# A fourth group of query weights ahead of the first weighted sum, loaded into two row buffers

## The reference

```python
q = (xt @ w_query).reshape(T, PEER_HEADS, 2, PEER_KEY_DIM // 2)   # 256 tokens, 8 heads, 2 x 128
s = jnp.einsum('thcd,hckd->thck', q, sub_keys)                    # 128 keys per half
s_top, i_top = lax.top_k(s, PEER_TOPK)                            # 16 of each half
...
g_s, g_pos = lax.top_k(cand, PEER_TOPK)                           # 16 of the 256 sums
g = jax.nn.softmax(g_s, -1)
# per token, head and choice: one row of expert_u and one of expert_v, 1024 numbers each
h = gelu(einsum('td,thkd->thk', xb, expert_u[eb]))
y = einsum('thk,thkd->td', g * h, expert_v[eb])
```

## Time and profile before

| | |
|---|---|
| median of the runs | 960.07 us |
| profiled execution | 959.62 us, its span 957.8 us |
| PE busy | 761.8 us (80%) |
| DVE busy | 593.0 us (62%) |
| ACT busy | 426.3 us (45%) |
| POOL busy | 300.8 us (31%) |
| mean granted TensorE clock | 0.839 |
| bytes moved by DMA | 335.33 MB |

### The profile page before, as it was taken

How to read it: one execution, slowest core, us unless ns; L and a number is a source line. 1 busy time by engine, 2 the same in 40 slices (tenths; PEclk the granted TensorE clock), 3 DMA queues, 4 the chain that set the end, 5 groups by cost and what they waited for, 6 DMA issues and landing times.

```text
span 957.8 us, 11712 instructions
## 1 busy us (share of the span) xinstructions
PE 761.8 (80%) x4022; PEld 352.5 (37%) x4026; DVE 593.0 (62%) x1424; ACT 426.3 (45%) x1179; POOL 300.8 (31%) x296
## 2 busy tenths in 40 slices
PE   7999999998888989979695757676867665767664
PEld 6876755665633435433131404141411111111110
DVE  1615340643779878868566655677667766767555
ACT  1144213542268967965343424354443434334333
POOL 0010021000334634544333334344433433343430
PEclk9999999999979997989796869697976777566667
DMA  7533253625799999999999999999999999999993
GB/s 280 238 119 122 100 230 144 257 85 231 280 420 420 420 422 401 420 420 423 420 422 422 421 421 422 421 419 422 421 420 423 420 419 423 421 421 420 420 421 151
DMA packets 45645, 335.33 MB, mean 350 GB/s; under 512 B 6033, under 2 KB 6033, under 8 KB 9105
## 3 DMA queue, kind: packets, MB, share of 16 engines
q0 software_dynamic: 37152, 268.45, 67.6%
q1 hardware_dynamic: 8432, 66.13, 17.5%
HBM read 333.51 MB, written 1.05 MB: 349 GB/s over the span
## 4 chain that ended last, share of the span: by engine, by line
DMA 45%; PE 36%; DVE 9%; ACT 5%; issue 3%; POOL 2%; SPq 0%; POOLq 0%; DVEq 0%; ACTq 0%
DMA late<-in_uv,eidx 27%; DMA ring<-in_uv,eidx 16%; PE ps L715 7%; PE ps L1052 7%; PE ps L700 5%; PE ps L839 4%; PE ps L881 4%; ACT late L1101 3%; DVE late L1804 2%; DVE ring L1804 2%; DMA late<-in_uv,apart 2%; ACT L1101 1%; PE ps L983 1%; POOL late L1903 1%; PE ps L950 1%
## 5 line engine op out<-in xcount | busy, mean ns | idle before, releaser
L1101 ACT ACTIVATE late<-late 128x1 f32<-128x1 f32 (+3 forms) x787 | 221.8, 285 | 337.0 <-DVE late L1804 315.0
L1052 PE MATMUL ps<-late 64*64 64x512 f32 x960 | 168.2, 789 | 77.4 <-ACT late L1101 73.8
L1052 PE MATMUL ps<-ring,late 64*64 64x512 f32 x928 | 162.0, 783 | 82.6 <-ACT late L1101 81.6
L1903 POOL DMA_INDIRECT late<-in_uv,eidx x118 | 130.7, 1107 | 249.5 <-PE ps L1052 183.9
L1804 DVE CUSTOM_DVE_ANT_0 late<-late,x_sb 128x1024 f32<-128x1024 f32 x120 | 147.0, 1225 | 92.7 <-DMA late<-in_uv,eidx 90.8
L1804 DVE CUSTOM_DVE_ANT_0 ring<-ring,x_sb 128x1024 f32<-128x1024 f32 x116 | 142.1, 1225 | 88.3 <-DMA ring<-in_uv,eidx 86.6
L1903 POOL DMA_INDIRECT ring<-in_uv,eidx x116 | 127.6, 1100 | 179.6 <-PE ps L1052 171.1
L1101 ACT ACT_TABLE_LOAD x82 | 105.2, 1283 | 11.8 <-PE ps L700 10.3
L1052 PEld LDWEIGHTS ps<-ring,late 64*64 64x64 f32 x928 | 29.3, 155 | 187.9 <-ACT late L1101 172.8
L1052 PEld LDWEIGHTS ps<-late 64*64 64x64 f32 x960 | 30.9, 156 | 179.5 <-ACT late L1101 161.1
L1101 ACT ACTIVATE tmp<-ps 128x512 f32<-128x512 f32 (+4 forms) x86 | 43.3, 507 | 94.6 <-PE ps L700 41.5
(11 more groups left out here) (254 smaller groups left out, 756.4 us busy)
## 6 DMA issues: line engine op xcount, KB each, us to landing
wring<-in_wts SPq DMA_DIRECT2D x21, 2048.0 KB, 11.4
wring<-in_wts SPq DMA_DIRECT2D x2, 1428.0 KB, 5.7
wring<-in_wts SPq DMA_DIRECT2D x2, 1388.0 KB, 6.3
ring<-in_wts SPq DMA_DIRECT2D x1, 2048.0 KB, 10.3
lnw<-in_ln SPq DMA_DIRECT2D x4, 512.0 KB, 12.5
late<-in_uv,eidx POOLq DMA_INDIRECT x118
ring<-in_uv,eidx POOLq DMA_INDIRECT x116
wring<-in_wts SPq DMA_DIRECT2D x3, 512.0 KB, 7.5
```

The costliest lines, as they stand in the source:

```text
L1052: last = mm(o[t][n * HD:(n + 1) * HD, :], factor[tokens, :], values[tokens, n * 512:(n + 1) * 512], start=start, stop=stop, skip_group_che ...
L1101: return nc.scalar.activation(out, in_, func, **kw)
L1903: G.indirect_dma_start(row(slots[g]), None, uv, bass.IndirectOffsetOnAxis(eidx[:, u % 2, k:k + 1], 0)).then_inc(row_here[slots[g]], 16)
```

## The change

Heads 4 and 5 become one group, (2, 0, 2), and `EARLY` becomes 4, so this group is multiplied ahead of `weighted(0)` too. Its weights no longer pass through `wring`: SP loads them into the whole of `ring2` (buffers 4 and 5), and POOL waits for the end of their multiplication, `("q", 0, OWN_HOME)`, before it issues row 6, the first one into `ring2`; `SLOT_ORDER` makes these two buffers the last of each eight up to g = 160. The two groups left, heads 6 and 7, stand at steps 25 and 42. The list of pieces is one shorter: piece 18 is now heads 6 and 7, piece 19 the first of block 1's output projection.

```diff
-QUERIES = [[(0, 0, 1), (0, 1, 1), (1, 0, 2), (2, 0, 1), (2, 1, 1), (3, 0, 1), (3, 1, 1)], [(n, 0, 2) for n in range(4)]]
-EARLY = 3
+QUERIES = [[(0, 0, 1), (0, 1, 1), (1, 0, 2), (2, 0, 2), (3, 0, 1), (3, 1, 1)], [(n, 0, 2) for n in range(4)]]
+EARLY = 4
+OWN_HOME = 3
+SLOT_ORDER = [0, 1, 2, 3, 6, 7, 4, 5]
...
-    for n, k in enumerate((14, 25, 36, 47)):
+    for n, k in enumerate((25, 42)):
         queries(0, EARLY + n, k, 1, 3)
...
-        slots = [g % RING0 if g < SWITCH else (g - SWITCH + RING0) % RING for g in range(NT * STEPS)]
+        slots = [SLOT_ORDER[g % RING0] if g < SWITCH else (g - SWITCH + RING0) % RING for g in range(NT * STEPS)]
...
-            order += [(18 + n, ("q", i, max(g for g, group in enumerate(QUERIES[i]) if group[0] == n))) for n in range(4)]
+            order += [(18 + n, ("q", i, max(g for g, group in enumerate(QUERIES[i]) if group[0] == n))) for n in range(4) if (i, n) != (0, 2)]
...
+                if k == 19:
+                    sp.wait_ge(sq_ready, NT + 1)
+                    await_full(sp, "qT", 1, 3)
+                    sp.dma_start(ring2[:, :], wts[:, starts[20]:starts[21]]).then_inc(wq_here, 16)
...
-                    if first == 0:
+                    if (i, n) == (0, OWN_HOME):
+                        pe.wait_ge(wq_here, 16)
+                        query[0] = ring2[:, :].rearrange("p (k n) -> p k n", k=KD)
+                    elif first == 0:
                         query[0] = next_piece()
...
+                if g == 4:
+                    await_full(pool, "z", 1, 1)
                 if g == 6:
-                    await_full(pool, "z", 1, 1)
+                    await_full(pool, "q", 0, OWN_HOME)
```

More of the change, by code:

```diff
@@ L478, in layer @@
         wz_here = sem("wz_here")
+        wq_here = sem("wq_here")
         first_step = sem("first_step")
```

## The result

The changed kernel takes 974.94 us, median of 4 runs (973.56 to 976.16), beside 960.37 for the kernel before in the same comparison: a ratio of 1.0157, 95% interval 1.0143 to 1.0171. That is 14.6 us slower. The profiled execution took 975.58, its span 973.7, which is 15.9 us more than before.

What follows compares the result with a forecast made beforehand. It took DMA bytes to bound the kernel from 250 us on; 4.9 (queues dry) + 8.9 (ramp) - 1.5 (clock) - 0.7 (dent) = 11.6 us on 959.62 gave 971.2, stated as 971.5, range 966 to 976 (55%).

Steps and rivals of the forecast that it cites:

- What bounds it: From 250 us on, the kernel ends when its bytes are through; DMA engines move about 420 GB/s.
- more than 421 GB/s anywhere: Sign of a wrong prediction: the DMA engines finding a rate above 421 GB/s at any place.
- The load: SP's load into ring2 behind piece 18: issued at 250.9 us, landing at about 270.1.
- turns of equal bytes: Alternative for SP's and POOL's queues sharing DMA: weights land at 274 us, sum 4 us higher; not taken.
- T: End of heads 4 and 5's queries on PE: 280.0 us, bounds 276.7 and 284.2, queries taking 9.8 us.
- The queues dry: Start of loop: queued bytes through at 277.6 us, row 6's bytes begin at 282.5; 4.9 us idle.
- The ramp: Rows 8 to 11 issued 7.4, 14.7, 18.9 and 20.6 us behind T; 8.9 us of DMA idle.
- I take 1.5: Taken off the ramp: second and third sums and scores partly at full clock, 1.5 of about 3 us.
- The half of the dent: DMA dent at 375 to 386 us, 1.4 us in all, half of it expected back.
- Row 12: Sign in the changed profile: row 12's dot product about 14 us later than before.
- Free by cover: Queries out of steps 14 and 36, output projection's first piece, buffer order and gate's wait at row 4 cost nothing.
- Nothing lost: Rival, 10%: the pauses at the loop's start stay covered, needing T = 267.9; 959 to 961 us.

Runs made afterwards that it cites:

- before_scores_ahead: Kernel before, with only block 1's compressed scores moved from between the first two sums to ahead of the first; 960.56 us, ratio 0.9998.
- warm_wait: Changed kernel plus 40 spare 128x128 matmuls on PE in its wait for the weights; 972.13 us, ratio 1.0121.
- buffer_order_alone: Kernel before, with only the change's order of buffers and the gate's wait at row 4; 960.22 us, ratio 0.9997.
- early_load: Changed kernel with SP's load into ring2 moved ahead of piece 18's wait; 963.24 us, ratio 1.0025.
- scores_in_wait: Changed kernel with block 1's compressed scores moved from step 0 into PE's wait for the weights; 970.21 us, ratio 1.0097.
- ahead_through_wring: Kernel before, with heads 4 and 5 multiplied ahead as one group, weights still through wring, no gather held; 967.01 us, ratio 1.0062.

## Why the prediction was right

The direction, the mechanism and the place hold; the size was 14.6 us where 11.6 was forecast (975 against 971.5).

- *What bounds it.* Right: bytes behind 250 us set the end, and the missing 16.2 us of transfer are the 15.9 us of the span. before_scores_ahead shows the other side of it. One sign of being wrong was met by the letter, "more than 421 GB/s anywhere": from 262 to 276 the changed kernel moves 426, with SP's load beside the rows. That is 0.2 us of work and moves nothing in the sum; 421 is the rate of the long stretch, not the highest that is seen.
- *The load.* Forecast at 250.9 and landed at 270.1; it was 249.5 and 269.6 with the loop 1.4 us earlier, so 0.9 us late. By the measured shares this was close. From 258 to 268 SP's queue (q1) again had about two thirds of the engines; behind each queue stand its packets, its MB and its share:

```profile
q1 hardware_dynamic: 197, 2.79, 65.2%
q0 software_dynamic: 203, 1.48, 35.1%
```

The rule of the Trainium skill, DMA: Bandwidth & Descriptors, "Queues, rings and completion order", that each DMA engine takes turns between its queues by the packet, agrees with this if one counts the profile's packets (which need not be what that page calls a packet): the two queues moved nearly the same number, 197 and 203 here, 109 and 108 before. But SP's packets are about twice as large, 14.2 KB against 7.3 on average here and 16.4 against 7.1 before, so even turns give SP two thirds of the bytes. The landing that the prediction worked out for turns of equal bytes would have been 3 us too late.

- *T.* Forecast 280.0, measured 280.1, in the loop's own time 1.5 us late: 0.9 from the landing, most of the rest from the queries, 10.2 us instead of 9.8. That these two figures lie so near is in part luck. The 8.4 us that the prediction took as the full-clock time hold a pause of 0.9 us that is no work; without it such queries take 7.3. And the clock cost 2.9 us, not 1.4: about half of the rows ran at the lower level and not a quarter (granted 0.50 from 270 to 274, 0.54 to 276, 1.00 behind it). The two errors cancel to 0.4 us.
- *The queues dry* at 277.6 and fed again at 282.5: measured about 276.6 (131 GB/s in the two us from 276) and about 282.7. This pause is 6.1 us where the sum had 4.9, for T was late by 1.5 in the loop's own time.
- *The ramp.* Issues of rows 8, 9, 10 and 11 forecast 7.4, 14.7, 18.9 and 20.6 us behind T, measured 8.0, 16.3, 20.6 and 22.3. The form was right and it was 1.7 us longer, mostly since the compressed scores ran at about 0.50 from their start: 7.0 us instead of 5.9. Idle in it by the prediction's own way of adding are then 10.6 us instead of 8.9, and 10.1 are missed from 284 to 304.
- *The step that failed* is the one taken off the ramp, "I take 1.5", for a better clock behind the queries. The clock was worse: 0.50 from 286 to 302. In warm_wait PE is busy nearly all the time from 258 to 277 and the granted clock is 0.50 again from 283 on. The half of the dent, 0.7, did not come back either: the place of the old dent is full (422 and 419 GB/s over 360 to 400), but 340 to 360 has 406, and from 304 to 400 it is 416 in all against 415 before.
- *The size.* In the profiled execution 11.6 us were forecast and 16.2 are missing. Of the 4.6 us between, 1.2 are the first pause, 2.7 the ramp (the 1.5 taken off it and 1.2 by which it was longer) and 0.7 the dent. The direction and the places came from the mechanism and not from luck; the size fell short in each of these three terms.
- *Row 12.* Its dot product was to come about 14 us later than before; it came 21.1 us later (315.1 against 294.0). The sign was badly chosen: the start of the loop moves with T, which moved 20.2 us, while the end moves only by the bytes missed.
- *Free by cover.* Right for the order of the buffers (buffer_order_alone). The queries out of steps 14 and 36 returned nothing that shows in 304 to 400.
- *The rivals.* "Nothing lost" needed T = 267.9. early_load has T = 267.3, with a loop that starts 0.5 us ahead of that of before, and still missed 8.7 us, since 2.10 MB of the cover had gone out early and the ramp was slow. Only with the faster ramp do the 5.0 us show as a gain. What I had taken as decided by T alone is decided by T, by the ramp and by how many bytes are left as cover.

Two things stay open: what limits scores_in_wait from 304 to 400 us, and what the half clock alone costs in the ramp. The scores take 7.0 us between the sums and 3.7 in the wait, but no run keeps them in their place at the full clock.

## What to carry to other kernels

Where a stream of transfers is the bound, look at who has bytes in the queues in each microsecond of a start or a change of phase: work put ahead of the first release of a buffer costs nothing only as long as queued bytes cover it, and here the other queue's weights were that cover. A load that is meant for an idle time has to stand ahead of every wait of its issuing engine that ends later than that time; one load moved on SP was worth 12 of 14.6 us. A shorter ramp is worth something only where the queues run dry: the same move of 32 matmul rows was worth 4 us in early_load and nothing in the kernel before.

## What I had not expected of the hardware

In early_load the granted clock was 0.78 over 268 to 272 us and 0.50 over 272 to 280, though PE had been busy with queries almost without a pause until 269; what stood between were waits of 0.7 and 1.6 us. The first sum and the one behind it took 1.98 us each instead of 1.09:

```profile
268.03 1.13 PE L901 MATMUL ps<-sk,tmp 128*128 128x128 f32 x8 [0.73 <-issue]
270.75 1.98 PE L1062 MATMUL ps<-x_sb,late 64*64 64x512 f32 x8 [1.59 <-ACT late L1111]
272.84 1.98 PE L1062 MATMUL ps<-late 64*64 64x512 f32 x8
```

The same queries also took 8.4 us in the profiled execution before, in two pieces with 0.9 us between them, and 7.3 without a gap in the changed kernel, early_load and others. ahead_through_wring has a gap of 0.5 us at the same place. The profile names nothing that PE waited for in it.
